# Mixture-of-experts weight loads: those of the run-time items begun by ScalarE's queue in place of SyncE's

## The chip, the core and the metric

The kernel runs on one core of a Trainium2 chip. The metric is device microseconds of one execution; before the change three runs gave a median of 2016.62 us. Five engines work side by side, each on its own list of instructions and in that list's order: TensorE (PE, its weight loads are listed as PEld), VectorE (DVE), ScalarE (ACT), GpSimd (POOL) and SyncE (SP). They meet at semaphores. Weights come from HBM by DMA; an engine begins a transfer with an instruction of its list, and the transfer's landing raises a semaphore.

## The reference, cut to what matters

The program is a model of three layers on 256 tokens of width 1024: a first layer with a state-space mixer, a sparse attention and a mixture of experts, and two layers with attention and a feed-forward part. The change touches only the experts of the first layer. There are 32 of them, and each token goes to two:

```python
for e in range(N_EXPERTS):
    he = jax.nn.silu(t @ w_g[e]) * (t @ w_u[e])
    out = out + combine[:, e:e + 1] * (he @ w_d[e])
```

`w_g` and `w_u` of an expert are 1024 x 256 each and stand together in `egu` (2 MB); `w_d` is 256 x 1024 in `edn` (1 MB). Which tokens an expert gets is known only at run time.

## The kernel before

**Items.** The 512 (token, expert) positions are sorted by expert. An item is at most 32 positions of one expert (`CAP`). Items 0 to 31 are fixed: item e is the first 32 positions of expert e. Items 32 to 46 are the run-time ones: they take the further positions of experts that have more than 32. Which expert such an item belongs to is in `over_expert_i`, and whether its weights differ from those that the previous run-time item used is in `over_fresh_i`; both are written by VectorE (`route_dve` at 6). A run-time item without positions, or of the same expert as the one before it, has fresh 0, and its two transfers are issued with that as their condition: they move nothing and count as landed.

**Order.** `ORDER` (line 54 ff.) is 0, 1, 2, 3, then pairs of fixed items with a run-time item behind each: 4, 5, 32, 6, 7, 33, 8, 9, 34, and so on. Behind the pairs (12, 13) and (22, 23) stand two run-time items: 12, 13, 36, 37, 14, 15, 38 and 22, 23, 42, 43, 24, 25, 44. It ends 28, 29, 46, 30, 31. "Step i" is what PE does at place i of this order.

**A step of PE.** At line 1201 it multiplies 32 rows with the item's 2 MB gate and up weights (64 matmuls; the semaphore `moe_h` counts them done). Then it turns the item before (line 1209), adds item i-3 into the sum over experts (line 1186, which needs the copy that ScalarE makes of its output, `moe_yev`) and multiplies item i-2 with its 1 MB down weights (line 1226, semaphore `moe_y`). Line 1201 waits for the gate and up weights to have landed (`gu_landed`), line 1226 for the down weights (`dn_landed`).

**ScalarE** in a step: the Silu of the item (line 1780, behind `moe_h`) and the copy of the output of item i-2 (line 1786, behind `moe_y`). It begins no DMA.

**Buffers.** There are four buffers for gate and up weights, which lie in arena, ring (two) and hn, and four for down weights in ring. Fixed items from 4 on use numbers 0, 1, 2 by turns; run-time items all use number 3, the one in hn. `BEFORE[i]` is the place in the order of the item that had the same buffer last.

**Who begins the loads.** SyncE alone, in one list (lines 579 to 594). At place i it reads the run-time item's expert and condition into registers (`value_load`, lines 586 and 587), waits for `moe_h` of `BEFORE[i]`, begins the gate and up load (line 555), then waits for `moe_y` of `BEFORE[i - 2]` and begins the down load of place i-2 (line 559). The list is strictly in order. The part that the change rewrites is this:

```python
sp.wait_ge(s["moe_h"], BEFORE[i] + 1)
load_gate_up(i, *expert[i])
if i >= 6:
    sp.wait_ge(s["moe_y"], BEFORE[i - 2] + 1)
    load_down(i - 2, *expert[i - 2])
```

Of the kernel before, what the change touches and what calls it, by code (L numbers as in the profile page):

```python
# [16 lines left out]
I32 = mybir.dt.int32  # L17
# [5 lines left out]
P = 128  # L23
# [19 lines left out]
NE = NG * EPG  # L43
# [7 lines left out]
ITEMS = NE + OVER  # L51


def item_order():

    first, pairs = 4, (NE - 4) // 2
    order, over = list(range(first)), NE
    for pair in range(pairs):
        order += [first + 2 * pair, first + 2 * pair + 1]
        for _ in range(pair < pairs - 1) if pair not in (4, 9) else range(2):  # L60
            order.append(over)
            over += 1
    assert over == ITEMS and len(order) == ITEMS
    return order


ORDER = item_order()
BUFFER = [item if item < 4 else 3 if item >= NE else (item - 4) % 3 for item in ORDER]
USE = [BUFFER[:i + 1].count(b) for i, b in enumerate(BUFFER)]
BEFORE = [max((j for j in range(i) if BUFFER[j] == b), default=None) for i, b in enumerate(BUFFER)]  # L70
LAST_OVER = max(i for i, item in enumerate(ORDER) if item >= NE)

KVG = 4
QL, KVL, RD, ND = 384, 256, 32, 64
# [135 lines left out]
def build(nc, dr):  # L210

    with ExitStack() as ctx:
# [3 lines left out]
        def sem(name):  # L216
            return ctx.enter_context(nc.semaphore(name))
# [31 lines left out]
        def slot(s, w=SLOTW):  # L249
            return ring[:, s * SLOTW:s * SLOTW + w]  # L250

        def w_down(q):

            return ring[:, 2 * SLOTW + q * SLOTW // 2:2 * SLOTW + (q + 1) * SLOTW // 2]
# [31 lines left out]
        gu_landed = [sem(f"gate_up{i}_landed") for i in range(4)]  # L286
        dn_landed = [sem(f"down{i}_landed") for i in range(4)]
# [17 lines left out]
        s = {n: sem(n) for n in names}  # L305
# [94 lines left out]
        offset_i, over_offset_i, over_expert_i, over_fresh_i = pl(NE), pl(OVER), pl(OVER), pl(OVER)  # L400
# [5 lines left out]
        def w_gate_up(q):  # L406

            return (gu_arena, slot(1), slot(0), hn[:, :, :].rearrange("p k t -> p (k t)"))[q]
# [77 lines left out]
        def _(sp):  # L486
            used = [0] * NSLOT

            def stream(trips, plan):

                per = {sl: sum(e[1] == sl for e in plan) for _, sl, _ in plan}
                for x, (name, sl, chunk) in enumerate(plan):
                    nth[name, chunk(0)] = used[sl] + sum(e[1] == sl for e in plan[:x]) + 1

                def body(i):
                    for x, (name, sl, chunk) in enumerate(plan):
                        before = sum(e[1] == sl for e in plan[:x])

                        sp.wait_ge(slot_free[sl], i * per[sl] + (used[sl] + before + 1))
                        sp.dma_start(slot(sl, STREAMS[name][1]), dr[name][bass.ts(chunk(i), P), :]) \  # L500
                            .then_inc(slot_landed[sl], 16)
                if trips > 1:
                    with sp.Fori(0, trips) as i:
                        body(i)
                else:
                    body(0)
                for _, sl, _ in plan:
                    used[sl] += trips
# [41 lines left out]
            stream(2, [("wo", 4, c2(0)), ("wo", 5, c2(1))])  # L550


            def load_gate_up(i, e, fresh=None):
                b = BUFFER[i]
                sp.dma_start(w_gate_up(b), dr["egu"][bass.ts(e, P), :], cond=fresh).then_inc(gu_landed[b], 16)

            def load_down(i, e, fresh=None):
                b = BUFFER[i]
                sp.dma_start(w_down(b), dr["edn"][bass.ts(e, P), :], cond=fresh).then_inc(dn_landed[b], 16)

            sp.wait_ge(phase, 3 * (MOE_PHASE - 2))
            load_gate_up(0, 0)
            sp.wait_ge(slot_free[1], used[1] + 1)
            load_gate_up(1, 1)
            sp.wait_ge(slot_free[2], used[2] + 1)
            for i in range(2):
                load_down(i, i)
            sp.wait_ge(slot_free[3], used[3] + 1)
            for i in range(2, 4):
                load_down(i, i)  # L570
            sp.wait_ge(slot_free[0], used[0] + 1)
            load_gate_up(2, 2)
            sp.wait_ge(phase, 3 * (MOE_PHASE - 1))
            sp.dma_start(iota, dr["iota"]).then_inc(s["moe_iota"], 16)
            sp.wait_ge(s["tok_mm"], 1)
            load_gate_up(3, 3)

            expert = {}
            for i in range(4, ITEMS + 2):
                if i < ITEMS:  # L580
                    item = ORDER[i]
                    if item == NE:
                        sp.wait_ge(s["route_dve"], 6)
                    if item >= NE:
                        over = slice(item - NE, item - NE + 1)
                        expert[i] = (sp.value_load(over_expert_i.bitcast(I32)[0:1, over], min_val=0, max_val=NE - 1),
                                     sp.value_load(over_fresh_i.bitcast(I32)[0:1, over], min_val=0, max_val=1))
                    else:
                        expert[i] = item, None
                    sp.wait_ge(s["moe_h"], BEFORE[i] + 1)  # L590
                    load_gate_up(i, *expert[i])
                if i >= 6:
                    sp.wait_ge(s["moe_y"], BEFORE[i - 2] + 1)
                    load_down(i - 2, *expert[i - 2])
            sp.wait_ge(s["moe_y"], ITEMS)

            def up_stream(l):
# [45 lines left out]
            out = dr["out"].rearrange("p (k t) -> p k t", k=KD)  # L643
# [852 lines left out]
        def _(act_e):  # L1496
# [24 lines left out]
            def shifted_half(part, shift, layer):  # L1521

                for k in range(KD):
                    act_e.wait_ge(s["hn_scaled"], n["hn_scaled"] + k + 1)
                    x = hn[:, k, part * T:(part + 1) * T]
                    fn(x, x, ACT.Identity, bias=ada[layer][:, shift + k, part:part + 1]).then_inc(s["hn_ready"], 1)
                n["hn_scaled"] += KD
# [244 lines left out]
            for dst, src in ((pos_rows, bank[6]), (w_rows, bank[7])):  # L1772
                fn(dst, src[:, :], ACT.Copy).then_inc(s["moe_rows_ev"], 1)

            for i in range(ITEMS + 2):
                if i < ITEMS:
                    act_e.wait_ge(s["moe_h"], i + 1)
                    if i >= 2:
                        act_e.wait_ge(s["moe_he"], i - 1)
                    fn(hsil[:, i % 2, :], bank[i % 2][:, 0:64], ACT.Silu).then_inc(s["moe_silu"], 1)  # L1780
                if i >= 2:
                    v = i - 2
                    act_e.wait_ge(s["moe_y"], v + 1)
                    if v >= 2:
                        act_e.wait_ge(s["moe_sum"], v - 1)
                    fn(y_sb[v % 2], bank[6 + v % 2][:, 0:T], ACT.Copy).then_inc(s["moe_yev"], 1)
                if i == ITEMS - 1:
                    shifted_half(1, 0, 1)
            for k in range(KD):
# [183 lines left out]
        def _(ve):  # L1973
# [610 lines left out]
            for i in range(ITEMS + 2):  # L2584
# [30 lines left out]
                if i == ITEMS - 2:  # L2615
                    ve.wait_ge(s["moe_h"], LAST_OVER + 1)
                    for k in range(KD):
# [318 lines left out]
```

## Time and profile before

| | before |
|---|---|
| median of 3 runs | 2016.62 us (2016.15 to 2019.36) |
| profiled execution, its own time | 2014.35 us |
| its span in the trace | 2012.5 us |
| granted TensorE clock, mean | 0.978 |
| PE busy | 1854.1 us (92%) |
| DVE busy | 1035.4 us (51%) |
| ACT busy | 551.9 us (27%) |
| DMA moved | 345.06 MB, mean 171 GB/s |

The experts run from about 585 us (first matmul of line 1201) to 864 us of the span. The span is shorter than the execution's own time by 1.85 us, the time around it. All times in the rows below are microseconds from the start of the span.

### The profile page before, as it was taken

How to read it: one execution, taken by the hardware profiler on the slowest of the kernel's cores; microseconds unless marked ns; L12 is line 12 of the kernel's file. 1: busy time of each engine (PE TensorE's matmuls, PEld its weight loads, DVE VectorE, ACT ScalarE, POOL GpSimd, SP SyncE). 2: the span in 40 equal slices, each digit the busy share in tenths (PEclk: the TensorE clock that was granted, in tenths of full speed). 3: DMA queues.
4: the chain of work that ended last, by engine and by line, in shares of the span. 5: the costliest groups of instructions: out<-in, count | busy, mean ns of one | idle time of the engine just before them, and what ended most of it. 6: DMA issues, size and time to landing. Idle time of an engine off the chain costs nothing.

```text
span 2012.5 us, 32990 instructions
## 1 busy us (share of the span) xinstructions
PE 1854.1 (92%) x12610; PEld 1352.0 (67%) x12610; DVE 1035.4 (51%) x2332; ACT 551.9 (27%) x1185; POOL 54.4 (3%) x76
## 2 busy tenths in 40 slices
PE   6999999999977777799999899999999899999998
PEld 4878788758755566554564588888444465778886
DVE  3366573387442222344687877776888326333311
ACT  3333400171130011031472333332000236244310
POOL 0000000000000000000000011111000010000000
PEclk8999999999998999999999999999999999999999
DMA  9445483414459896930204122222764030144451
GB/s 372 172 190 205 169 355 152 177 71 188 200 236 422 345 378 281 409 147 0 84 2 177 54 84 84 83 92 111 295 258 194 12 102 7 43 148 156 162 194 50
DMA packets 38530, 345.06 MB, mean 171 GB/s; under 512 B 4231, under 2 KB 9102, under 8 KB 10382
## 3 DMA queue, kind: packets, MB, share of 16 engines
q1 hardware_dynamic: 38414, 343.45, 43.4%
q8 instruction: 80, 1.31, 0.3%
q14 instruction: 36, 0.29, 0.1%
HBM read 380.14 MB, written 1.05 MB: 189 GB/s over the span
## 4 chain that ended last, share of the span: by engine, by line
PE 86%; issue 5%; DVE 4%; DMA 2%; ACT 1%; PEld 1%; DVEq 0%; SPq 0%; ACTq 0%; PEldq 0%
PE bank L681 50%; PE bank L1437 13%; PE bank L1201 5%; PE bank L1186 2%; PE bank L1226 2%; PE bank L802 2%; PE bank L1402 1%; PE bank L1311 1%; PE bank L1319 1%; DMA ring<-in_ada 1%; PE bank L1162 1%; PE bank L907 1%; PE bank L1409 1%; DMA hn<-in_egu 1%; DVE ring L2130 1%
## 5 line engine op out<-in xcount | busy, mean ns | idle before, releaser
L681 PE MATMUL bank<-hn,ring 128*128 128x256 f32 (+2 forms) x2080 | 515.3, 407 | 9.6 <-ACT hn L1535 8.0
L681 PE MATMUL bank<-arena,ring 128*128 128x256 f32 (+2 forms) x1600 | 467.3, 449 | 17.4 <-issue 13.7
L681 PEld LDWEIGHTS bank<-hn,ring 128*128 128x128 f32 (+1 forms) x2080 | 395.5, 191 | 119.7 <-issue 68.4
L681 PEld LDWEIGHTS bank<-arena,ring 128*128 128x128 f32 (+1 forms) x1600 | 297.7, 188 | 180.3 <-issue 147.9
L1437 PE MATMUL bank<-ring 128*128 128x256 f32 x704 | 160.7, 381 | 1.2 <-DVE ring L2757 0.6
L1437 PEld LDWEIGHTS bank<-ring 128*128 128x128 f32 x704 | 133.6, 191 | 21.7 <-issue 2.1
L2017 DVE SCALAR_TENSOR_TENSOR bank<-ring,c_rows 128x1024 f32<-128x1024 f32 x96 | 118.1, 1230 | 21.6 <-DMA ring<-in_ada 16.7
L1437 PE MATMUL bank<-hn,ring 128*128 128x256 f32 x528 | 123.0, 383 | 3.8 <-ACT hn L1877 3.8
L2017 DVE SCALAR_TENSOR_TENSOR ring<-ring,c_rows 128x1024 f32<-128x1024 f32 x96 | 117.2, 1220 | 0.0
L1515 ACT ACTIVATE hn<-resid 128x256 f32<-128x256 f32 (+1 forms) x48 | 22.6, 485 | 336.4 <-DVE resid L2108 336.4
L1437 PEld LDWEIGHTS bank<-hn,ring 128*128 128x128 f32 x528 | 101.3, 192 | 18.6 <-issue 4.6
L2590 DVE COPY ring<-bank 128x64 f32<-128x64 f32 x47 | 10.6, 225 | 182.3 <-PE bank L1209 182.3
L2108 DVE SCALAR_TENSOR_TENSOR resid<-bank,ada,resid 128x256 f32<-128x256 f32 x56 | 25.6, 481 | 137.9 <-PE bank L681 137.8
L2757 DVE TENSOR_TENSOR ring<-ring,bank 128x256 f32<-128x256 f32 x154 | 59.3, 419 | 55.1 <-PE bank L1437 50.6
L2803 DVE SCALAR_TENSOR_TENSOR ring<-bank,cols,ring 128x255 f32<-128x255 f32 x88 | 40.4, 480 | 91.8 <-ACT ring L1913 88.1
L1890 ACT ACTIVATE ring<-ring,cols 128x512 f32<-128x512 f32 x44 | 35.8, 813 | 151.7 <-DVE ring L2757 151.7
L1201 PE MATMUL bank<-ring,arena 128*32 128x128 f32 x1280 | 48.9, 308 | 30.8 <-issue 30.3
L802 PEld LDWEIGHTS bank<-consts,ring 128*128 128x128 f32 x416 | 45.4, 141 | 40.1 <-DVE ring L2151 31.8
L2752 DVE SCALAR_TENSOR_TENSOR ring<-ring,cols 128x510 f32<-128x510 f32 x88 | 63.1, 748 | 15.6 <-issue 11.4
L1562 ACT ACTIVATE ring<-bank 128x512 f32<-128x512 f32 (+1 forms) x128 | 59.3, 518 | 41.4 <-PE bank L802 41.2
L1201 PEld LDWEIGHTS bank<-ring,arena 128*32 128x32 f32 x1280 | 43.1, 125 | 37.7 <-issue 36.5
L2135 DVE TENSOR_REDUCE ring<-bank 128x2 f32<-128x1024 f32 (+1 forms) x48 | 50.3, 1047 | 28.8 <-PE bank L1402 19.0
(434 smaller groups left out, 2098.8 us busy)
## 6 DMA issues: line engine op xcount, KB each, us to landing
ring<-in_ada SPq DMA_DIRECT2D x28, 2048.0 KB, 7.9
ring<-in_edn SPq DMA_DIRECT2D x47, 1024.0 KB, 15.2
ring<-in_up SPq DMA_DIRECT2D x44, 1024.0 KB, 4.8
ring<-in_egu SPq DMA_DIRECT2D x20, 2048.0 KB, 16.5
hn<-in_egu SPq DMA_DIRECT2D x16, 2048.0 KB
arena<-in_egu SPq DMA_DIRECT2D x11, 2048.0 KB, 18.4
ring<-in_down SPq DMA_DIRECT2D x16, 1408.0 KB, 9.3
ring<-in_adat SPq DMA_DIRECT2D x8, 2048.0 KB, 11.8
```

Source lines behind the costliest of these rows:

```text
L681: last = mm(out, lhs(i), rhs(i), start=i == 0, stop=i == k - 1)
L802: last = tr(bank[4 + e][:, x * P:(x + 1) * P], probs[t % 3][:, e, c:c + P], ident)
L1186: last = mm(moe_sum(2 * q + m), y_sb[v % 2][rows, m * P:(m + 1) * P], s_t[v % 2][rows, :], start=v == 0 and m == 0, stop=v == ITEMS - 1 an ...
L1201: last = mm(bank[x][CAP * q:CAP * q + CAP, 0:P], x_t[x][:, k, :] if i else xs[:, k, 0:CAP], w_gate_up(BUFFER[i])[:, k * 512 + q * P:k * 51 ...
L1226: last = mm(bank[6 + x][CAP * q:CAP * q + CAP, 0:T], he_t[:, x, k * CAP:(k + 1) * CAP], w_down(BUFFER[v])[:, k * D + q * T:k * D + (q + 1) ...
L1437: last = mm(bank[4 * q + b][:, 0:T], lhs[:, k, :], rhs(k), start=k == 0, stop=k == 3)
L1562: fn(probs_t[t % 2][:, e, 0:w], banks[:, 4 + e, 0:w], ACT.Copy).then_inc(s["att_PT"], 1)
L2017: V.scalar_tensor_tensor(products, w, 1.0, c_row if layer == 0 else c_rows[:, v, :], ALU.mult, ALU.mult, accum_out=sums[x][:, b, v:v + 1])
L2135: V.tensor_reduce(nmax[p % 3][:, :, 0:1], banks[:, x:x + 2, 0:u.w].rearrange("p e (b k) -> p e b k", b=1), AX.X, ALU.max, negate=True).the ...
L2752: V.scalar_tensor_tensor(aa, uu, cols[:, ds(j + (cw + tap * 2 * FB + x * FB), 1)], aa, ALU.mult, ALU.add)
L2757: V.tensor_tensor(out, one, other, ALU.add).then_inc(s["up_added"], 1)
L2803: V.scalar_tensor_tensor(aa, uu, cols[:, ds(j + (cw + tap * 2 * FB + x * FB), 1)], aa, ALU.mult, ALU.add)
```

## The change

SyncE's list now has the fixed items alone: for e from 4 on, the gate and up load of item e behind `moe_h` of the item that had its buffer, then the down load of item e-1 behind `moe_y`. The loads of the 15 run-time items are in ScalarE's list. There the function `over_load` reads expert and condition into ScalarE's registers and begins the transfer, with no wait of its own but that for the routing before the first: it stands behind the Silu of the place that had buffer 3 last (gate and up, which has waited for that place's `moe_h`), and behind the copy of that place's output (down, which has waited for its `moe_y`). Each of the two loads reads both registers anew. Conditions, buffers, sizes and the order of the items are as before. Line numbers shift by up to nine (the Silu is line 1779 now, the copy line 1789).

```diff
-LAST_OVER = max(i for i, item in enumerate(ORDER) if item >= NE)
+AT = {item: i for i, item in enumerate(ORDER)}
+LAST_OVER = AT[ITEMS - 1]
...
-            expert = {}
-            for i in range(4, ITEMS + 2):
-                if i < ITEMS:
-                    item = ORDER[i]
-                    if item == NE:
-                        sp.wait_ge(s["route_dve"], 6)
-                    if item >= NE:
-                        over = slice(item - NE, item - NE + 1)
-                        expert[i] = (sp.value_load(over_expert_i.bitcast(I32)[0:1, over], min_val=0, max_val=NE - 1),
-                                     sp.value_load(over_fresh_i.bitcast(I32)[0:1, over], min_val=0, max_val=1))
-                    else:
-                        expert[i] = item, None
-                    sp.wait_ge(s["moe_h"], BEFORE[i] + 1)
-                    load_gate_up(i, *expert[i])
-                if i >= 6:
-                    sp.wait_ge(s["moe_y"], BEFORE[i - 2] + 1)
-                    load_down(i - 2, *expert[i - 2])
+            for e in range(4, NE + 1):
+                if e < NE:
+                    sp.wait_ge(s["moe_h"], BEFORE[AT[e]] + 1)
+                    load_gate_up(e)
+                if e >= 5:
+                    sp.wait_ge(s["moe_y"], BEFORE[AT[e - 1]] + 1)
+                    load_down(e - 1)
...
+            def over_load(item, out, name, landed):
+
+                over = slice(item - NE, item - NE + 1)
+                e = act_e.value_load(over_expert_i.bitcast(I32)[0:1, over], min_val=0, max_val=NE - 1)
+                fresh = act_e.value_load(over_fresh_i.bitcast(I32)[0:1, over], min_val=0, max_val=1)
+                act_e.dma_start(out, dr[name][bass.ts(e, P), :], cond=fresh).then_inc(landed, 16)
+
+            next_over = {BEFORE[AT[item]]: item for item in range(NE, ITEMS)}
             for i in range(ITEMS + 2):
                 if i < ITEMS:
...
                     fn(hsil[:, i % 2, :], bank[i % 2][:, 0:64], ACT.Silu).then_inc(s["moe_silu"], 1)
+                    if i in next_over:
+                        if next_over[i] == NE:
+                            act_e.wait_ge(s["route_dve"], 6)
+                        over_load(next_over[i], w_gate_up(3), "egu", gu_landed[3])
...
                     fn(y_sb[v % 2], bank[6 + v % 2][:, 0:T], ACT.Copy).then_inc(s["moe_yev"], 1)
+                    if v in next_over:
+                        over_load(next_over[v], w_down(3), "edn", dn_landed[3])
```

SyncE before, from the load of item 36 (condition read at lines 586 and 587, then the wait for `moe_h`) through item 37's to item 14's; hn is the run-time buffer, `egu` the gate and up weights, `edn` the down weights:

```order
L555 DMA hn<-in_egu 128x4096
L559 DMA ring<-in_edn 128x2048 [waits moe_y]
L586 TENSOR_LOAD ring
L586 ISA x2
L587 TENSOR_LOAD ring
L587 ISA x2
L555 ISA [waits moe_h]
L555 DMA hn<-in_egu 128x4096
L559 DMA ring<-in_edn 128x2048 [waits moe_y]
L555 DMA ring<-in_egu 128x4096 [waits moe_h]
```

SyncE now, the same stretch: the loads of items 13 to 15 follow one another.

```order
L556 DMA arena<-in_egu 128x4096 [waits moe_h]
L560 DMA ring<-in_edn 128x2048 [waits moe_y]
L556 DMA ring<-in_egu 128x4096 [waits moe_h]
L560 DMA ring<-in_edn 128x2048 [waits moe_y]
L556 DMA ring<-in_egu 128x4096 [waits moe_h]
```

The register reads, the two waits and the two conditional DMAs of each run-time item have left SyncE's list; between two fixed items nothing else stands in it.

ScalarE before, two steps of the same stretch (line 1780 is the Silu, line 1786 the copy of the output):

```order
L1780 ACTIVATE ring<-bank 128x64 [waits moe_he,moe_h]
L1786 ACTIVATE arena<-bank 128x256 [waits moe_sum,moe_y]
L1780 ACTIVATE ring<-bank 128x64 [waits moe_he,moe_h]
```

ScalarE now, from the Silu of item 36 (line 1779) through the load of item 37's gate and up weights to that of a run-time item's down weights behind a copy (line 1789):

```order
L1779 ACTIVATE ring<-bank 128x64 [waits moe_he,moe_h]
L1769 TENSOR_LOAD ring
L1769 ISA x2
L1770 TENSOR_LOAD ring
L1770 ISA x2
L1771 ISA
L1771 DMA hn<-in_egu 128x4096
L1789 ACTIVATE arena<-bank 128x256 [waits moe_sum,moe_y]
```

What SyncE lost stands here between a Silu and the next copy, or between a copy and the next Silu, twice for each run-time item.

## Rows read from the trace of the kernel before

**Rows 1.** The page's chain that ended last, shares by line

```profile
PE bank L681 50%; PE bank L1437 13%; PE bank L1201 5%; PE bank L1186 2%; PE bank L1226 2%; PE bank L802 2%; PE bank L1402 1%; PE bank L1311 1%; PE bank L1319 1%; DMA ring<-in_ada 1%; PE bank L1162 1%; PE bank L907 1%; PE bank L1409 1%; DMA hn<-in_egu 1%; DVE ring L2130 1%
```

**Rows 2.** Stretches of the experts: busy by engine, granted clock, DMA share, GB/s

```profile
588.00:684.00 96.00, 71.51 (x1631) 55.04 (x1634) 25.03 (x73) 11.86 (x35) 6.45 (x16) 0.93 1.00 413
684.00:703.00 19.00, 13.58 (x312) 10.38 (x311) 4.62 (x12) 1.83 (x6) 1.21 (x3) 0.89 0.60 226
703.00:730.00 27.00, 20.53 (x447) 16.42 (x450) 6.16 (x16) 2.44 (x8) 1.61 (x4) 0.82 0.81 334
730.00:771.00 41.00, 32.61 (x810) 24.68 (x801) 12.36 (x32) 4.49 (x15) 3.23 (x8) 1.00 1.01 424
771.00:794.30 23.30, 16.80 (x418) 13.06 (x417) 6.18 (x16) 2.82 (x9) 1.61 (x4) 0.93 0.59 238
794.30:814.00 19.70, 14.57 (x328) 11.95 (x332) 4.64 (x12) 1.83 (x6) 1.21 (x3) 0.85 0.70 286
```

**Rows 3.** SyncE in order of time: DMA issues (start, us, engine, line, tile)

```profile
671.14 0.09 SPq L555 DMA_DIRECT2D hn<-in_egu  x1
...
691.72 0.08 SPq L555 DMA_DIRECT2D hn<-in_egu  x1
...
692.23 1.31 SPq L555 DMA_DIRECT2D ring<-in_egu  x1
...
768.09 0.09 SPq L555 DMA_DIRECT2D hn<-in_egu  x1
...
783.13 0.08 SPq L555 DMA_DIRECT2D hn<-in_egu  x1
```

**Rows 4.** PE in order of time: steps of items 13, 14, 24, 31 [idle before]

```profile
683.90 2.50 PE L1201 MATMUL bank<-arena 128*32 128x128 f32 x64 [3.17 <-issue]
...
703.04 3.20 PE L1201 MATMUL bank<-ring,arena 128*32 128x128 f32 x64 [3.83 <-issue]
...
794.34 3.62 PE L1201 MATMUL bank<-ring,arena 128*32 128x128 f32 x64 [5.01 <-issue]
...
851.51 1.80 PE L1201 MATMUL bank<-arena 128*32 128x128 f32 x57
```

**Rows 5.** PE in order of time where its weights lay ready (items 40 to 22, 42, 43, 28 to 30)

```profile
751.26 0.96 PE L1201 MATMUL bank<-hn,arena 128*32 128x128 f32 x26 [1.95 <-issue]
...
754.33 1.91 PE L1201 MATMUL bank<-ring,arena 128*32 128x128 f32 x58
...
771.20 0.31 PE L1201 MATMUL bank<-arena 128*32 128x128 f32 x3
...
780.87 1.93 PE L1201 MATMUL bank<-hn,arena 128*32 128x128 f32 x64
...
783.91 1.07 PE L1226 MATMUL bank<-ring 128*32 128x256 f32 x16
784.80 1.93 PE L1201 MATMUL bank<-hn,arena 128*32 128x128 f32 x64
...
830.08 1.93 PE L1201 MATMUL bank<-arena 128*32 128x128 f32 x64
...
846.14 1.25 PE L1201 MATMUL bank<-ring,arena 128*32 128x128 f32 x34
```

**Rows 6.** DMA queues from 585 to 866 us: packets, MB, share of 16 engines

```profile
q8 instruction: 39, 0.64, 0.9%
```

**Rows 7.** SyncE's register reads and conditional loads (ns min/median/max, first and last start)

```profile
L586 SPq TENSOR_LOAD <-ring x15: 266/269/478, 591.7 to 825.4; - x15
L587 SPq TENSOR_LOAD <-ring x15: 264/266/285, 592.5 to 826.0; - x15
L555 SPq DMA_DIRECT2D hn<-in_egu x16: 79/89/348, 560.3 to 827.2; - x16
```

**Rows 8.** What ScalarE waited for, 588 to 864 us (total us, times, longest)

```profile
ACT ring L1780 <- PE bank L1201: 131.9, 45, 8.2
ACT arena L1786 <- PE bank L1226: 109.1, 46, 4.6
```

More of the change, by code:

```diff
@@ L550, in _, with load_gate_up, load_down @@
             stream(2, [("wo", 4, c2(0)), ("wo", 5, c2(1))])
[L553 to L559, printed above, removed]
+            def load_gate_up(e):
+                b = BUFFER[AT[e]]
+                sp.dma_start(w_gate_up(b), dr["egu"][bass.ts(e, P), :]).then_inc(gu_landed[b], 16)
+            def load_down(e):
+                b = BUFFER[AT[e]]
+                sp.dma_start(w_down(b), dr["edn"][bass.ts(e, P), :]).then_inc(dn_landed[b], 16)
             sp.wait_ge(phase, 3 * (MOE_PHASE - 2))
-            load_gate_up(0, 0)
+            load_gate_up(0)
             sp.wait_ge(slot_free[1], used[1] + 1)
-            load_gate_up(1, 1)
+            load_gate_up(1)
             sp.wait_ge(slot_free[2], used[2] + 1)
             for i in range(2):
-                load_down(i, i)
+                load_down(i)
             sp.wait_ge(slot_free[3], used[3] + 1)
             for i in range(2, 4):
-                load_down(i, i)
+                load_down(i)
             sp.wait_ge(slot_free[0], used[0] + 1)
-            load_gate_up(2, 2)
+            load_gate_up(2)
             sp.wait_ge(phase, 3 * (MOE_PHASE - 1))
@@ L575, in _ @@
             sp.wait_ge(s["tok_mm"], 1)
-            load_gate_up(3, 3)
-            expert = {}
-            for i in range(4, ITEMS + 2):
-                if i < ITEMS:
-                    item = ORDER[i]
-                    if item == NE:
-                        sp.wait_ge(s["route_dve"], 6)
-                    if item >= NE:
-                        over = slice(item - NE, item - NE + 1)
-                        expert[i] = (sp.value_load(over_expert_i.bitcast(I32)[0:1, over], min_val=0, max_val=NE - 1),
-                                     sp.value_load(over_fresh_i.bitcast(I32)[0:1, over], min_val=0, max_val=1))
-                    else:
-                        expert[i] = item, None
-                    sp.wait_ge(s["moe_h"], BEFORE[i] + 1)
-                    load_gate_up(i, *expert[i])
-                if i >= 6:
-                    sp.wait_ge(s["moe_y"], BEFORE[i - 2] + 1)
-                    load_down(i - 2, *expert[i - 2])
+            load_gate_up(3)
+            for e in range(4, NE + 1):
[5 more added lines that the diff above has]
+                    load_down(e - 1)
             sp.wait_ge(s["moe_y"], ITEMS)
```

## The prediction

> **What bounds the kernel now.** I read the chain that ended last first. Matmuls of other lines hold most of it; the experts' lines 1201, 1186 and 1226 hold 9% and the loads of `egu` into hn another 1% [rows 1]. So the change can move only the 279 us of the experts. Within them I read the stretches, by the DMA share. Up to 684 us it is 1.00 at 413 GB/s: the transfers never stop, and three run-time items (32, 33, 35) are fresh there and load real weights, which shows in their issues of 0.35 us against some 0.09 us for a skipped one [rows 2, 7]. From 684 us on no run-time item loads anything, yet the share falls to 0.60, 0.81, 0.59 and 0.70, with one full stretch between at 1.01 and 424 GB/s [rows 2].
>
> SyncE's own times name the reason. After the skipped load of item 36 at 671.14 us its list stands until 691.72 us, when it issues the skipped load of item 37, and 0.5 us later the 2 MB of item 14 go out [rows 3]. Item 37 uses the same buffer as item 36, one place before it, so SyncE waits for PE to do item 36, for a load that moves nothing, and item 14's load stands behind it although its own buffer came free at item 11, well before the step of item 13 at 683.90 us. The pair 42, 43 does the same from 768.09 to 783.13 us [rows 3]. PE then waits for weights: 3.83 us in front of item 14 and 5.01 us in front of item 24 [rows 4]. ("issue" there is a wait for a landing that the profile cannot name.) Those steps also run slowly: 3.62 us for 64 matmuls behind the 5.01 us wait, in a stretch whose mean granted clock is 0.85 (part of it at the lower level, 1.2 GHz), against 1.91 us where the stretch has 1.00 (2.4 GHz) [rows 2, 4, 5].
>
> **What the removal is worth.** Two bounds come first. If the DMA queues stayed full until the last byte, the missing share would come back: 19.0 x 0.40 + 27.0 x 0.19 + 23.3 x 0.41 + 19.7 x 0.30 = 7.6 + 5.1 + 9.6 + 5.9 = 28.2 us [rows 2]. The other bound is PE's pace when its weights lie ready. Where the transfers are full it needs 16.87 us for items 20, 21, 41 (754.33 to 771.20) and 16.06 us for 28, 29, 46 (830.08 to 846.14), so (16.87 + 16.06) / 6 = 5.49 us a step; with the transfers empty it needs 3.93 us (780.87 to 784.80) [rows 5].
>
> The difference lies in gaps in the middle of an item's matmuls, such as the 1.95 us in front of the 26 matmuls at 751.26 us, where no landing can be missing [rows 5]. I read them as PE waiting for its own instructions: 39 packets of instructions, 0.64 MB, were fetched among the weights [rows 6], 16 KB each, and PE's 208 instructions a step (64 + 8 + 16 + 16 matmuls, each with a weight load) are some 9,800 in 47 items, one such packet per 256. The Trainium skill (Runtime: NRT & Kernel Launch, Instruction fetch mechanics) says that crossing a 16 KiB block costs one tail bump and is mostly hidden. The gap of 1.95 us speaks against it in this stage; by that rule a step would cost 3.93 us throughout, which is the second rival below.
>
> Now the sum, from the step of item 13 at 683.90 us, the last that the full transfers of the first stretch feed, to item 31 at 851.51 us: 167.6 us for 29 steps [rows 4]. A fixed item's loads are 128 x 4096 and 128 x 2048 numbers of 4 bytes, 3.15 MB, at 424 GB/s 7.42 us, a pair 14.84 us [rows 2]. While these move, PE does 14.84 / 5.49 = 2.70 steps; the rest of a group goes at 3.93 us. A group of two fixed items and one run-time item is then 14.84 + 0.30 x 3.93 = 16.0 us, one with two run-time items 14.84 + 1.30 x 3.93 = 19.9 us. In order: items 13, 36, 37 while a backlog still moves, 3 x 5.49 = 16.5; seven groups of three, 112.0; the group 22, 23, 42, 43, 19.9; item 30, 5.5. Together 153.9 us against 167.6, a gain of **13.7 us**. In this sum PE's pace is late next, not the transfers (14.84 of every 16.0 us).
>
> **What ScalarE's queue costs the first stretch.** There the transfers are full, so an earlier issue buys nothing, and three fresh items now load from a second queue beside SyncE's. How two queues share the engines no row of before shows. At best the bytes arrive in the old order: 0. At worst each of the three gate and up loads gets half the rate and delays its item by its own length once more, 3 x 2.10 MB / 424 GB/s = 3 x 4.95 = 14.8 us. I take the length of one down load, 1.05 MB or **2.5 us**, because the work in the queues is the same and full in either order, and only item 35's down load can newly get ahead of item 13's weights. That leaves 13.7 - 2.5 = **11.2 us**.
>
> **What ScalarE itself pays.** 15 items x 2 loads x 2 register reads. One read is 0.27 us, and from the first read's start to the second's it is 0.6 to 0.8 us on SyncE [rows 7]; two reads and the issue of 0.09 to 0.35 us make 1.3 to 2.0 us, 30 times 39 to 60 us. ScalarE waits 131.9 + 109.1 = 241.0 us of this stage [rows 8], so it has the time in total. Step by step: in the tight step from 780.87 us the matmuls end at 782.80; the Silu stands there, and the copy waits for line 1226, which ends at 784.98 [rows 5]. A load between the two has 2.2 us less the Silu. If it takes longer, the copy is late, but PE wants it in the next step only, behind that step's matmuls at 784.80 + 1.93 us, some 1.7 us later. I cost it at nothing up to about 3.5 us (2.2 + 1.7 less the Silu and the copy). On SyncE the removed reads and issues cost nothing before, since it waited anyhow; taking them off is no gain of its own. At the two double places ScalarE's load of item 37 begins after a Silu and two reads, some 1.5 us later than SyncE's 691.72 us, which had its registers ready; PE wanted item 37 1.7 us after that, so 0 to 0.5 us twice, inside the rounding.
>
> Sum: the profiled execution took 2014.35 us, 2014.35 - 11.2 = 2003.2; that execution is 2.3 us below the median of 2016.62, by which I give the prediction: **2005.4 us**.
>
> **Bounds of this case.** With 5.35 us a step (28, 29, 46 alone), and no delay: 16.05 + 7 x 15.7 + 19.7 + 5.35 = 151.0, a gain of 16.6 us, 2000.0 us. With 5.62 us a step throughout (20, 21, 41) and the 2.5 us lost: 29 x 5.62 = 163.0, a gain of 2.1 us, 2014.5 us.
>
> **The rivals.** *The transfers become the limit.* With a shallower queue the instruction gaps go, and steps approach 3.93 us; seven groups would need 14.84 us each and the gain is the whole 28.2 us: **1988.4 us**. For it: the 3.93 us steps exist while the queues are empty. Against: the transfers would be full again, which is just when the gaps stand. 10%.
>
> *Nothing comes of it.* The fixed items' loads find other waits in the same list (the down load of item e-1 waits for a `moe_y`), or the fresh items lose at half rate what the rest gains (13.7 - 14.8): **2016.6 us**, give or take 4. The Trainium skill speaks for this (DMA: Bandwidth & Descriptors, Issuing engines are not separate DMA queues): issuing on several engines saves only the sequencer's time to issue. By it the worth would be the 0.1 to 1.3 us issues. The 20.6 us between two issues of SyncE [rows 3] are not issue time but a wait in order, which the rule does not speak of. 15%.
>
> *Slower: ScalarE becomes late.* If a load on it holds the list well over 3.5 us (a register read there waits for more than on SyncE, or the issue stalls as the one of 1.31 us did [rows 3]), the copy comes late, then line 1186 and all behind it. At 5 us that is 15 x 1.5 = 22.5 us, against 11.2 gained: **2027.9 us**. It decides from 3.5 + 11.2 / 15 = 4.2 us. For it: no row shows a read or a DMA on ScalarE. Against: SyncE's rows give half of that. 7%.
>
> **Chances.** The forecast has 68%, the rivals 10, 15 and 7. A measurement of this kernel can tell about 0.2%, 4 us. Faster by more: the forecast less its slow end, and the first rival, 78%. Within: 15%. Slower: 7%. The range of 1995 to 2015 us holds the forecast with both bounds and nearly all of the second rival's better half; outside lie the first rival, the third and some of the second, 20%.
>
> **What would show it.** Right: SyncE's issues no longer stand 15 to 20 us at the double places, item 14's load goes out before 684 us, the waits of 3.83 and 5.01 us in front of items 14 and 24 are gone, the DMA share of 684 to 840 us is even, at about 0.9, and the gaps inside the items remain. The steps up to item 13 are the same or 2 to 3 us late. Wrong: waits for landings in front of fresh items that grow by several us; a first entry of ScalarE among those that PE's line 1186 waits for; steps that stay at 5.8 us with the loads long landed, which would mean that PE's pace, not the blocked list, was the cause all along.

## The result, and the profile after

The changed kernel has a median of 1993.21 us in four runs (1992.81 to 1997.18); the kernel before, beside it on the same chip, has 2016.38 us (2013.8 to 2019.36). The ratio is 0.9889, with an interval of 0.987 to 0.9908: 23.2 us less. The forecast was 2005.4 us, 11.2 us less, with a range of 1995 to 2015 us. The sign was right, the gain was twice the forecast, and the time lies 1.8 us outside the range. In a second comparison on another chip (below) the changed kernel had 1993.29 us and the kernel before 2013.26 us, 20.0 us less.

The profiled execution of the changed kernel spans 1990.9 us against 2012.5 us. Nearly all of the difference lies in the experts. I cut each trace at the same four instructions: the first matmul of the experts, the first of item 13's step, the first of item 31's step, and the end of the last down matmul.

| us, profiled execution | before | after |
|---|---|---|
| up to the first expert matmul | 585.05 | 583.71 |
| items 0 to 13 | 98.85 | 98.81 |
| item 13 to item 31 | 167.61 | 148.50 |
| item 31 to the end of the experts | 12.04 | 10.67 |
| after the experts | 1148.97 | 1149.24 |

The page's chain of the changed kernel, shares by line (answers to [rows 1]; the experts' lines are now 1192, 1177 and 1217), and the DMA queue q10 over the whole span (packets, MB, share). The load of `egu` into hn is gone from the chain, and q10, which is ScalarE's and had no row before, carries 9.44 MB: the weights of the three run-time items that are fresh, 3 x 3.15 MB.

```profile
PE bank L672 49%; PE bank L1428 13%; PE bank L1192 5%; PE bank L1177 3%; PE bank L1217 2%; PE bank L793 2%; PEld bank L672 2%; PE bank L1393 1%; PE bank L1302 1%; PE bank L1310 1%; DMA ring<-in_ada 1%; PE bank L1153 1%; PE bank L1400 1%; PE bank L898 1%; DVE ring L2135 1%
...
q10 hardware_dynamic: 864, 9.44, 1.1%
```

The stretches of the experts in the changed kernel, with the columns of [rows 2] (the last three are granted clock, DMA share and GB/s):

```profile
586.70:682.50 95.80, 70.81 (x1627) 55.20 (x1626) 25.01 (x73) 11.83 (x35) 6.42 (x16) 0.91 1.01 419
682.50:703.00 20.50, 19.57 (x487) 15.72 (x488) 6.17 (x16) 2.43 (x8) 1.60 (x4) 0.92 1.01 424
703.00:730.00 27.00, 22.52 (x515) 16.77 (x510) 7.74 (x20) 3.04 (x10) 2.01 (x5) 0.94 1.01 424
730.00:771.00 41.00, 34.01 (x829) 25.86 (x818) 12.37 (x32) 4.86 (x16) 3.20 (x8) 1.00 0.99 406
771.00:794.70 23.70, 19.65 (x480) 14.91 (x483) 7.71 (x20) 2.65 (x9) 2.00 (x5) 1.00 0.90 368
794.70:841.70 47.00, 38.63 (x908) 28.32 (x900) 20.24 (x52) 8.70 (x26) 2.41 (x6) 1.00 0.68 267
```

The transfers stay full up to 771 us, where before the share had dropped to 0.60 at 684 us [rows 2]. PE is busy for 19.57 of the 20.5 us behind item 13, against 13.58 of 19.0.

SyncE in order of time (start, us, engine, line, tile): the loads of gate and up weights (`egu`) of items 14 to 16, the fixed items around the double place, and one load of down weights (`edn`).

```profile
659.08 0.33 SPq L560 DMA_DIRECT2D ring<-in_edn  x1
666.69 0.33 SPq L556 DMA_DIRECT2D ring<-in_egu  x1
...
676.73 0.33 SPq L556 DMA_DIRECT2D ring<-in_egu  x1
...
685.08 0.33 SPq L556 DMA_DIRECT2D arena<-in_egu  x1
```

They follow one another at 8 to 10 us, and from 655 to 698 us no two issues of SyncE are further apart than 7.6 us (659.08 to 666.69). Item 14's load goes out at 666.69 us, 15.8 us before item 13's step; in [rows 3] it went out at 692.23 us, 8.3 us after that step had begun.

PE in order of time, the first matmuls of the steps of items 13, 36, 37, 14 and 15, then of items 24 and 31 [idle before]:

```profile
682.52 2.52 PE L1192 MATMUL bank<-arena 128*32 128x128 f32 x64 [3.64 <-issue]
...
688.09 1.93 PE L1192 MATMUL bank<-hn,arena 128*32 128x128 f32 x64
...
692.03 1.93 PE L1192 MATMUL bank<-hn,arena 128*32 128x128 f32 x64
...
695.96 1.95 PE L1192 MATMUL bank<-ring,arena 128*32 128x128 f32 x64
...
699.92 0.39 PE L1192 MATMUL bank<-ring,arena 128*32 128x128 f32 x6
701.23 1.80 PE L1192 MATMUL bank<-ring,arena 128*32 128x128 f32 x57 [0.91 <-issue]
...
780.83 1.93 PE L1192 MATMUL bank<-ring,arena 128*32 128x128 f32 x64
...
831.02 1.80 PE L1192 MATMUL bank<-arena 128*32 128x128 f32 x57
```

The waits of 3.83 us before item 14 and 5.01 us before item 24 [rows 4] are gone: both steps begin without idle time (695.96 and 780.83 us). The step of item 13 still waits 3.64 us, as before (3.17). And steps 36, 37 and 14 follow at 3.94, 3.93 and 3.96 us, though the transfers are full beside them; the gap inside an item comes back at 701.23 us only. That pace is what the prediction had not foreseen.

### The profile page after: what moved, and what is told of

It is laid out like the page before. It is cut to its first block, busy times and chain, and to the rows that moved or that the text cites. A ratio compares the mean times of both kernels' runs of the same rounds, so it can differ in the third digit from the quotient of the medians.

```text
span 1990.9 us, 33082 instructions
## 1 busy us (share of the span) xinstructions
PE 1849.2 (93%) x12610; PEld 1348.9 (68%) x12610; DVE 1035.5 (52%) x2332; ACT 551.4 (28%) x1185; POOL 54.2 (3%) x76
## 3 DMA queue, kind: packets, MB, share of 16 engines
q10 hardware_dynamic: 864, 9.44, 1.1%
## 4 chain that ended last, share of the span: by engine, by line
PE 86%; issue 4%; DVE 4%; DMA 2%; PEld 2%; ACT 1%; DVEq 0%; SPq 0%; PEldq 0%; ACTq 0%
PE bank L672 49%; PE bank L1428 13%; PE bank L1192 5%; PE bank L1177 3%; PE bank L1217 2%; PE bank L793 2%; PEld bank L672 2%; PE bank L1393 1%; PE bank L1302 1%; PE bank L1310 1%; DMA ring<-in_ada 1%; PE bank L1153 1%; PE bank L1400 1%; PE bank L898 1%; DVE ring L2135 1%
## 5 line engine op out<-in xcount | busy, mean ns | idle before, releaser
L1428 PEld LDWEIGHTS bank<-ring 128*128 128x128 f32 x704 | 133.7, 191 | 21.6 <-issue 2.1
L2022 DVE SCALAR_TENSOR_TENSOR bank<-ring,c_rows 128x1024 f32<-128x1024 f32 x96 | 118.1, 1231 | 21.5 <-DMA ring<-in_ada 16.7
L1177 PE MATMUL bank<-ring,arena 32*128 32x256 f32 x752 | 57.6, 409 | 7.9 <-issue 5.7
L793 PE MATMUL bank<-consts,ring 128*128 128x128 f32 x416 | 58.8, 279 | 6.2 <-DVE ring L2156 6.2
```

Source lines behind the costliest of these rows:

```text
L793: last = tr(bank[4 + e][:, x * P:(x + 1) * P], probs[t % 3][:, e, c:c + P], ident)
L1177: last = mm(moe_sum(2 * q + m), y_sb[v % 2][rows, m * P:(m + 1) * P], s_t[v % 2][rows, :], start=v == 0 and m == 0, stop=v == ITEMS - 1 an ...
L1428: last = mm(bank[4 * q + b][:, 0:T], lhs[:, k, :], rhs(k), start=k == 0, stop=k == 3)
L2022: V.scalar_tensor_tensor(products, w, 1.0, c_row if layer == 0 else c_rows[:, v, :], ALU.mult, ALU.mult, accum_out=sums[x][:, b, v:v + 1])
```

## The experiments

The theory: SyncE's list in strict order was the cause. The loads of fixed items stood behind a run-time item's wait, and any list in which they don't gives the gain; ScalarE's queue as such gives none. The rivals: the second queue gives the gain (its own share of the DMA engines, or issue time saved); PE's pace is set by something that the change moved, not by waits for weights. Ratios are against the kernel before, run beside each group of experiments.

### The order without the second queue

Edit of the kernel before: SyncE begins every load, in the order in which the buffers come free.

```diff
-            for i in range(4, ITEMS + 2):
-                ...
+            ...
+            loads = sorted([(BEFORE[i], 0, ORDER[i] >= NE, i) for i in range(4, ITEMS)] +
+                           [(BEFORE[i] + 2, 1, ORDER[i] >= NE, i) for i in range(4, ITEMS)])
+            for _, down, over, i in loads:
+                ...
+                e, fresh = run_time(i) if over else (ORDER[i], None)
+                sp.wait_ge(s["moe_y" if down else "moe_h"], BEFORE[i] + 1)
+                (load_down if down else load_gate_up)(i, e, fresh)
```

> SyncE begins all loads, as in the kernel before, and ScalarE none; SyncE's list is sorted by the step in which each load's buffer comes free. Theory (the gain is that fixed loads no longer stand behind a run-time item's wait in one list): as fast as the changed kernel, 18 to 24 us under the kernel before (ratio 0.988 to 0.991), and no issue of SyncE 15 us late at the double places. Rival (a second queue beside SyncE's carries the bytes sooner): under 5 us gained.

Measured: 1997.45 us, ratio 0.9918 [0.9898, 0.9939], 16.9 us less and so just short of the expected 18 to 24. The experts take 259.1 us from the first matmul to the last, against 258.0 in the changed kernel and 278.5 before. SyncE in order of time (start, us, engine, line, tile), its loads of gate and up weights for items 14, 36, 15 and 37:

```profile
665.36 0.33 SPq L555 DMA_DIRECT2D ring<-in_egu  x1
...
677.76 0.10 SPq L555 DMA_DIRECT2D hn<-in_egu  x1
...
681.81 0.34 SPq L555 DMA_DIRECT2D ring<-in_egu  x1
...
695.80 0.09 SPq L555 DMA_DIRECT2D hn<-in_egu  x1
```

Item 14's load goes out at 665.36 us, 12 us before the skipped load of item 36 and 30 us before that of item 37. With one queue and the same instructions in another order, the experts are as short as with two, within 1.1 us. The second queue is not the cause.

### Half of the loads moved

Edit of the kernel before: ScalarE begins the run-time items' gate and up loads alone, or their down loads alone; the other half stays in SyncE's list at its old place.

```diff
-                    sp.wait_ge(s["moe_h"], BEFORE[i] + 1)
-                    load_gate_up(i, *expert[i])
-                if i >= 6:
+                    if not ACT_GATE(item):
+                        sp.wait_ge(s["moe_h"], BEFORE[i] + 1)
+                        load_gate_up(i, *expert[i])
+                if i >= 6 and not ACT_DOWN(ORDER[i - 2]):
...
```

Gate and up alone (`ACT_GATE` true for every run-time item, `ACT_DOWN` for none):

> ScalarE begins the run-time items' gate and up loads alone; their down loads stand in SyncE's list at their old place. Theory: items 14 and 24 no longer wait, but items 16 and 26 still do, since SyncE still stands for the output of item 36 (42) before it begins them: 10 to 18 us gained. Rival (gate and up loads on a second queue are what counts, 2 of every 3 MB): all of it, 20 us or more.

Measured: 2006.11 us, ratio 0.9949 [0.9931, 0.9968]; experts 271.2 us, in a profiled execution that lies 3.1 us above that median. Down alone:

> ScalarE begins the run-time items' down loads alone; their gate and up loads stand in SyncE's list at their old place. Theory: the wait for item 36 (42) in front of item 14 (24) stays, the later ones for items 16 and 26 go: 5 to 12 us gained. Rival: a third of the bytes, a third of the gain or less, under 7 us, and both waits stay.

Measured: 2008.65 us, ratio 0.997 [0.9959, 0.9981]; experts 275.1 us. SyncE in order of time around the double place, gate and up moved:

```profile
689.00 0.33 SPq L566 DMA_DIRECT2D ring<-in_egu  x1
706.73 1.59 SPq L570 DMA_DIRECT2D ring<-in_edn  x2
708.37 0.43 SPq L566 DMA_DIRECT2D arena<-in_egu  x1
```

and the same with the down loads moved:

```profile
671.51 0.09 SPq L566 DMA_DIRECT2D hn<-in_egu  x1
671.64 0.33 SPq L570 DMA_DIRECT2D ring<-in_edn  x1
694.54 0.09 SPq L566 DMA_DIRECT2D hn<-in_egu  x1
...
695.05 1.16 SPq L566 DMA_DIRECT2D ring<-in_egu  x2
```

In the first, the list stands from 689.00 to 706.73 us at the down load of item 37 (which waits for item 36's `moe_y`), and item 16's 2 MB go out behind it at 708.37 us. In the second it stands from 671.64 to 694.54 us at item 37's gate and up load, as before the change. Each half of a run-time item's loads holds the list by itself. PE then waits before items 16 and 26 in the first (4.72 and 4.86 us), and before items 14 and 24 in the second (5.12 and 5.16 us), as expected. The gains of the halves (8.3 us, less than the expected 10 to 18, and 5.7 us, which its rival allows too) add up to less than the whole: either wait that stays takes the DMA share down, to 0.68 from 683 to 720 us in the first and to 0.74 from 687 to 720 us in the second.

### Only the two double places

Edit: the loads of items 37 and 43 alone, the second of each double place, go to ScalarE; the other 13 run-time items stay with SyncE.

```diff
+def ACT_GATE(item):
+    return item in (NE + 5, NE + 11)
+def ACT_DOWN(item):
+    return item in (NE + 5, NE + 11)
```

> ScalarE begins the loads of items 37 and 43 alone, the second ones of the two double places; the other 13 run-time items stay with SyncE at their old place. None of the two is fresh, so ScalarE's queue moves nothing. Theory: the double places hold nearly all of the loss, 14 to 21 us gained. Rival (each run-time item's wait costs its share): 2 of 15, some 3 us.

Measured: 1997.57 us, ratio 0.9916 [0.9895, 0.9937]; experts 261.8 us. SyncE there (start, us, engine, line, tile), the loads of gate and up weights for items 36, 14 and 15:

```profile
669.28 0.09 SPq L566 DMA_DIRECT2D hn<-in_egu  x1
...
671.59 0.43 SPq L566 DMA_DIRECT2D ring<-in_egu  x1
...
687.85 0.33 SPq L566 DMA_DIRECT2D ring<-in_egu  x1
```

The queue of the weights over the experts (packets, MB, share):

```profile
q1 hardware_dynamic: 8928, 97.52, 91.4%
```

Four loads of the 30, none of which moves a byte, bring 278.5 - 261.8 = 16.7 us of the 20.5 us that the whole change takes from the experts (278.5 - 258.0). All bytes are still on SyncE's queue (97.52 MB on q1, no row for ScalarE's). So the place of four fifths of the gain is settled: the two double places. Which of the other waits hold the remaining 3.8 us is not shown.

### Hardly any weights

Edit, of the changed kernel and of the kernel before alike: from item 4 on a load takes 64 of 4096 columns (32 of 2048; 64 in ScalarE's down loads), so most expert weights are left out; instructions, waits and order are the same.

```diff
-sp.dma_start(w_gate_up(b), dr["egu"][bass.ts(e, P), :]) ...
+sp.dma_start(w_gate_up(b)[:, 0:WIDE(e, 64, 4096)], dr["egu"][bass.ts(e, P), 0:WIDE(e, 64, 4096)]) ...
...
```

> The changed kernel with its loads of experts from item 4 on cut to 64 and 32 of their columns (the rest of each buffer keeps what it held, so the experts' numbers are others): PE's work as before, next to no traffic beside it. Theory (the gaps inside the items' matmuls are PE's instructions coming late behind the weights): no gaps over 1 us, 3.9 to 4.1 us a step, the experts in about 190 us, 65 us less than the changed kernel. Rival (the gaps are PE's own): they stay, 5 us a step, some 240 us.

> The kernel before with the same loads cut in the same way. SyncE's list is blocked at the double places as ever. Theory: a load begun late lands within 3 us when nothing is queued, so items 14 and 24 wait 0 to 2 us and the experts take within 5 us of the changed kernel cut alike. Rival (the blocked list costs its 20 us wait by itself): 15 to 20 us more than that.

Measured, one run each: 1923.51 us (the changed kernel's order) and 1927.3 us (the order of before). The experts take 189.88 us in both; the 3.8 us between the two times lie outside them. One stretch of each, with the columns of [rows 2], the changed kernel's order first:

```profile
600.00:760.00 160.00, 160.00 (x4240) 127.78 (x4236) 65.25 (x169) 24.72 (x81) 16.02 (x40) 1.00 0.06 13
```

then the order of before:

```profile
600.00:760.00 160.00, 160.00 (x4224) 127.53 (x4220) 65.63 (x171) 24.72 (x82) 16.42 (x41) 1.00 0.06 12
```

SyncE in order of time in the order of before (the skipped loads of items 36 and 37, then item 14's load):

```profile
643.84 0.09 SPq L560 DMA_DIRECT2D hn<-in_egu  x1
...
655.62 0.08 SPq L560 DMA_DIRECT2D hn<-in_egu  x1
...
656.14 0.49 SPq L560 DMA_DIRECT2D ring<-in_egu  x1
```

Two things follow. With the DMA share at 0.06 every step takes 3.94 us and no gap over 1 us stands inside an item's matmuls; in the changed kernel there are 14 and a step takes 5.12 us. The gaps come from the traffic of weights. And SyncE's list still stands for 12 us at item 37 (643.84 to 655.62 us), yet PE never waits, because the small load that follows lands in time for item 14's step at 661.23 us. The blocked list costs only what the load behind it then lacks in time to land.

### ScalarE made slower

Edit of the changed kernel: four, or eight, register reads more before each of ScalarE's loads.

```diff
+                for _ in range(4):
+                    act_e.value_load(over_expert_i.bitcast(I32)[0:1, over], min_val=0, max_val=NE - 1)
```

> The changed kernel, with four more register reads in each of ScalarE's 30 loads, which then hold its list some 3.6 us each instead of 1.4. Theory (slack of about 3.5 us): within 3 us of the changed kernel. Rival (ScalarE's list is already on the path): 15 x 2.2 = 33 us more.

> The same with eight more reads, some 5.8 us each. Theory: the copy comes 2.3 us late in 15 steps, up to 35 us slower than the changed kernel, so slower than the kernel before too, and line 1177 waits for ScalarE. Rival (two outputs of slack hide that too): within 5 us of the changed kernel.

Measured: 1998.15 us with four, ratio 0.9912 [0.9888, 0.9936]; 2055.21 us with eight, ratio 1.0198 [1.0174, 1.0223]. From the end of the Silu to the end of the issue ScalarE is held for 1.46 us in the changed kernel (a load that moves data, from 616.25 us), 3.57 us with four reads more (the same load), 5.46 us with eight (a skipped one, from 753.74 us). What PE waited for over the experts (total us, times, longest), the changed kernel:

```profile
PE bank L1192 <- issue: 36.3, 23, 4.0
...
PE bank L1177 <- ACT arena L1789: 1.7, 2, 1.3
```

with four reads more:

```profile
PE bank L1192 <- DMA hn<-in_egu: 6.2, 1, 6.2
PE bank L1177 <- ACT arena L1791: 3.3, 5, 1.3
```

and with eight:

```profile
PE bank L1177 <- ACT arena L1791: 48.4, 15, 5.6
PE bank L1192 <- issue: 27.5, 9, 7.9
```

One such wait with eight more, in PE's order of time [idle before],

```profile
759.74 2.09 PE L1177 MATMUL bank<-ring,arena 32*128 32x256 f32 x16 [5.37 <-ACT arena L1791]
```

and the stretches on either side of its end (columns of [rows 2]):

```profile
751.00:759.70 8.70, 2.38 (x80) 1.86 (x72) 1.53 (x4) 0.62 (x3) 0.40 (x1) 0.88 0.96 363
759.70:764.00 4.30, 4.26 (x44) 2.51 (x48) 1.40 (x3) 0.34 (x2) 0.00 (x0) 0.50 0.25 103
```

So the rival of a late ScalarE is real, and it is steep. At 3.57 us a load PE's waits for the copy rise by 1.6 us in all, near the prediction's threshold of about 3.5 us. But the experts take 264.6 us, 6.6 more, and the kernel some 5 more, over the 3 us that were expected: PE also waits for the loads themselves, 6.2 us for the landing of a fresh one, and at the double places 1.55 us for item 37 and 2.88 us for item 43, whose skipped loads are issued some 0.15 us before their steps begin. At 5.46 us PE waits for the copy at 15 places, 48.4 us. In the one shown two loads stand in a row (ScalarE in order of time, the down load and the Silu behind it):

```profile
753.33 0.09 ACTq L1773 DMA_DIRECT2D ring<-in_edn  x1
753.52 0.22 ACT L1781 ACTIVATE ring<-bank 128x64 f32<-128x64 f32 x1 [5.70 <-PE bank L1192]
```

The Silu's matmuls had ended at 749.12 us; it begins only behind the down load, and the gate and up load behind it holds the copy until 759.30 us. Such a wait also costs TensorE its clock: in the 4.3 us behind it the granted clock is 0.50 (1.2 GHz), and line 1177 takes 2.09 us for what takes 1.15. The experts take 318.3 us, 60.3 more than in the changed kernel and far over the expected 35, at a mean granted clock of 0.85 against 0.95. The break-even lies between 3.57 and 5.46 us; it was not measured closer.

### Shorter rows

The gaps suggested that PE's instructions have to wait behind the weights' rows of 16 KB (8 KB in a down load). If so, shorter rows should let them through sooner. Edit of the changed kernel: each load of a fixed item cut into four (or two) DMAs by columns, rows of 4 (or 8) KB.

```diff
+                n = GU_PARTS[b]
+                for x in range(n):
+                    c = slice(x * SLOTW // n, (x + 1) * SLOTW // n)
+                    sp.dma_start(w_gate_up(b)[:, c], dr["egu"][bass.ts(e, P), c]).then_inc(gu_landed[b], 16)
...
```

> The changed kernel with SyncE's expert loads cut by columns: a gate and up load as four transfers of 4 KB rows in place of one of 16 KB rows, a down load as two of 4 KB in place of one of 8 KB; ScalarE's loads, bytes and order as they are. Theory (PE's instructions wait behind the rows that an engine has already taken up, so shorter rows let them through sooner): gaps over 1 us become fewer than the 14 of the changed kernel, 4.5 us a step from item 13 to 31 in place of 5.1, 5 to 15 us less than the changed kernel. Rival (the instructions wait for the bytes in front of them, whatever their cut): the same gaps, within 4 us of the changed kernel, or slower by the extra issues.

> The same with two transfers of 8 KB rows for a gate and up load and one of 8 KB rows, as it is, for a down load. Theory: about half of what the cut to 4 KB brings. Rival: no difference from the changed kernel.

> The changed kernel itself once more, beside the others of this call: 0.987 to 0.991 of the kernel before.

> SyncE's sorted list without ScalarE once more, on the same chip as the changed kernel. If ScalarE's second queue has a worth beside the order, the changed kernel is 3 to 5 us faster, all of it up to the step of item 14, where the fresh run-time items load; if the order is everything, both agree within 2 us.

Measured on one chip: rows of 4 KB 2003.24 us (0.9947 [0.993, 0.9964]), rows of 8 KB 1997.87 us (0.9921 [0.9904, 0.9937]), the changed kernel 1993.29 us (0.9903 [0.9887, 0.992]), SyncE alone in sorted order 1995.65 us (0.9909 [0.9892, 0.9925]). Gaps over 1 us inside an item's matmuls: 15 and 17 with shorter rows, 13 and 13 in the two others. The theory that the rows' length makes the gaps falls: shorter rows bring no fewer. They also move the bytes more slowly. The hardware queue over the second half of the experts (packets, MB, share), first with rows of 4 KB from 684 to 852 us:

```profile
q1 hardware_dynamic: 16050, 58.42, 89.3%
```

then the changed kernel from 684 to 842 us:

```profile
q1 hardware_dynamic: 5288, 56.95, 88.1%
```

58.42 MB in 168 us at a share of 89.3% are 389 GB/s of queue time, 56.95 MB in 158 us at 88.1% are 409: three times the packets, 5% less rate.

The repeats confirm the first comparison of order and queue. Experts: 259.1 us (changed) and 258.7 us (SyncE sorted). The 2.4 us between their medians lie behind the experts: 1148.7 against 1151.5 us; where they come in, the granted clock is 0.99 against 0.97 in the first traces of the two. That time varies among runs whose edits do not touch it: it is 1148.97 us in the kernel before and 1151.54 us with the two double places alone. Why is open.

## Why the prediction was right, and where it was wrong

**The mechanism held.** SyncE's list blocked by run-time loads that move nothing, at two double places: the order alone removes it (259.1 us against 258.0 for the experts), and four loads moved at those places take away four fifths of it. The rule of the Trainium skill that the prediction set against the gain (DMA: Bandwidth & Descriptors, Issuing engines are not separate DMA queues) agrees as far as it goes: a second issuing engine by itself changed the experts by 1.1 us or less. What the change bought was never issue time but a wait in order, as the prediction said.

**The signs named ahead.** SyncE's issues around the double place are 7.6 us apart at most instead of 20.6; item 14's load is out before 684 us; both waits are gone; the gaps remain (14 against 9). The DMA share from 682.5 to 841.7 us is (20.5 x 1.01 + 27 x 1.01 + 41 x 0.99 + 23.7 x 0.90 + 47 x 0.68) / 159.2 = 0.89, as forecast, but not even: full at first, 0.68 at the end. Full transfers do not mean that PE waited for them: from the step of item 13 to that of item 31 every idle time of PE over 0.1 us, 22.9 us in all, stands at one of the places of the gaps (below). PE's pace set the time there, as the sum had it.

**The term that was mis-sized: PE's pace.** From item 13 to item 31 the sum had 153.9 us and 148.5 were measured. By its own groups:

| group | forecast | after |
|---|---|---|
| items 13, 36, 37 | 16.5 | 13.44 |
| seven groups of three | 112.0 | 109.0 |
| items 22, 23, 42, 43 | 19.9 | 21.21 |
| item 30 | 5.5 | 4.83 |

The step that failed is "while a backlog still moves, 3 x 5.49": the 5.49 us were read from two places where PE had gone for some steps without a wait, and taken as what a step costs whenever the transfers are full. Behind the 3.64 us wait before item 13 PE went three steps at 3.93 to 3.96 us beside full transfers, and the gaps returned at 701.23 us. That one group is 3.1 of the 5.4 us; the seven groups give 3.0 more, since their pace too was a little better than the two that I had read (they range from 13.86 to 18.03 us; a group passes two or three of the places where gaps stand, so a reading over three steps scatters), and the other two about cancel (1.3 too few, 0.7 too many).

**The second queue in the first stretch, charged with 2.5 us, cost at most 1.** Items 0 to 13 took 98.81 us against 98.85, and 99.79 in the repeat. The fear was not unfounded: two queues with work do share the engines. The DMA queues from 601 to 612 us (packets, MB, share; q1 is SyncE's, q10 ScalarE's):

```profile
q1 hardware_dynamic: 223, 2.52, 53.9%
q10 hardware_dynamic: 144, 2.10, 44.9%
```

Item 32's gate and up weights landed at 612.54 us instead of 607.18, and its step began 9.0 us after the one before. But the bytes up to item 13 are the same and the queues were full throughout, so the delay was made up by item 13, where PE waits for the last of them in either kernel. That need not hold for every order: with the down loads alone on ScalarE the same stretch took 102.46 us, for a reason that is not shown.

**What was left out.** The tail behind item 31 is 1.4 us shorter, and the experts begin 1.3 us earlier, which the change cannot have caused. In sum: 11.2 forecast + 5.4 + 2.5 + 1.4 + 1.3 = 21.8, against 21.6 between the spans. The medians differ by 23.2, since the profiled execution of before stood 2.0 us below its median here and that of the changed kernel 0.4 us below its own.

**ScalarE.** The charge of nothing was right: PE's wait for the copy is 1.7 us in all, at two places, in both kernels, and the loads measured held ScalarE for 1.2 to 1.5 us, at or under the low end of the 1.3 to 2.0 forecast. At the double place (ScalarE in order of time, [idle before]) the load stands between the Silu and a copy that waited for PE anyhow:

```profile
690.09 0.22 ACT L1779 ACTIVATE ring<-bank 128x64 f32<-128x64 f32 x1 [1.36 <-PE bank L1192]
691.44 0.09 ACTq L1771 DMA_DIRECT2D hn<-in_egu  x1
692.28 0.38 ACT L1789 ACTIVATE arena<-bank 128x256 f32<-128x256 f32 x1 [1.97 <-PE bank L1217]
```

The slower rival's threshold of 3.5 us holds for the copy alone: at 3.57 us PE's waits for it rise by 1.6 us, but PE waits for the late loads themselves too, and the experts take 6.6 us more. Its price beyond was too low: 15 x (5.46 - 3.5) = 29 us by its formula, 60 measured. The formula charges one load a group, and in the place shown two in a row hold the copy; the lower clock behind the wait adds to it.

**The range** left out the rival in which the transfers become the limit (1988.4 us), and that rival did not come true: PE waited for none of them behind item 13. (The working calls its case of 3.93 us a step "the second rival"; it is the first in the list.) The fast bound of 2000.0 us had 151.0 us for items 13 to 31, built from the same pace, where 148.5 were measured; the rest of the miss lies outside that stretch and in the spread of executions, for which 1995 left too little room.

**The gaps.** That they come from weights' traffic is shown (none at a share of 0.06). That PE waits in them for its own instructions, as the prediction read them, their places show. PE's list is the same in all these kernels: 4890 matmuls in the experts, each with a weight load, over the 39 packets of instructions of [rows 6], so some 125 matmuls a packet, an estimate from these counts. In the twelve runs with full weights 140 gaps of over 1 us stand inside an item's matmuls. They fall on only 22 places of the list, 126 or 127 matmuls or a multiple of that apart, and each ends 1.2 to 1.6 us after a packet of instructions has arrived. The gap in item 15, with 57 matmuls left, stands in the changed kernel at 701.23 us and with the two double places alone here:

```profile
702.04 1.80 PE L1213 MATMUL bank<-ring,arena 128*32 128x128 f32 x57 [1.93 <-issue]
```

The Trainium skill (Runtime: NRT & Kernel Launch, Instruction fetch mechanics) calls a block's crossing mostly hidden, and the runs agree where the transfers are empty, 3.94 us a step throughout; beside full transfers they do not, a step takes 5.1 us. What holds the packets back there stays open; rows of 4 KB did not help.

## What to carry to other kernels

In an engine's list a load that moves nothing still takes its place and its wait; sort the list by when each buffer comes free, or give loads with another rhythm to an engine with idle time. Measure that idle time per step and not in total: here 3.6 us a load cost 5 to 7 us and 5.5 us cost 60 us. A pace read from steps in a steady stream does not hold right behind a wait; take it from steps with the same history.

## What the runs showed of the hardware

- Beside full weight transfers TensorE waited for its own instructions, mostly 1 to 2 us at a time, at places 126 or 127 matmuls (or a multiple) apart; with the transfers at a share of 0.06 it did not.
- A wait buys back time: after 3.64 us of idle PE went three steps at 3.93 to 3.96 us beside full transfers, where a steady stream needs 5.1 to 5.5. In the repeat (3.85 us of idle) and with the two double places alone (3.22 us) the next gap came in item 15 too. The run with eight reads more points the same way: with PE held 15 times by ScalarE, the gaps inside items fall from 14 to 2. So a wait can cost less than its length, because gaps that would have followed don't come.
- Two queues with work in them shared the engines almost evenly by bytes, 2.52 and 2.10 MB in 11 us.
- A load on ScalarE with two register reads held it for 1.2 us when skipped and 1.5 us when it moved data, in the two places measured.
- Rows of 4 KB moved at 5% less than rows of 16 and 8 KB, and the kernel took 10 us longer with them.
- Behind a wait of 5.37 us with PE busy for 2.38 of 8.7 us, the granted clock was 0.50 for the next 4.3 us.
